# One stream of w_in blocks over three stages of a decoder trunk, with the next part's first weights prepared in the part before

## The reference

```
xn = rmsnorm(h);  proj = xn @ w_in                # 1024 x (3072 gates | 3328 RWKV | 1024 S5 | 2048 z, 3072 xBC, 32 dt)
o_r = rwkv7(...) ; o_s = s5(...) @ w_out_s5 ; o_m = mamba2(...) @ w_out_mamba
h  += rmsnorm((sig(g_r)*o_r + sig(g_s)*o_s + sig(g_m)*o_m) @ w_out)
mem_k, mem_v = rmsnorm(mem) @ xa_wk, rmsnorm(mem) @ xa_wv          # 256 memory tokens, both are outputs
h  += rmsnorm(cross_attend(rmsnorm(h), mem_k, mem_v));  h += rmsnorm(relu(rmsnorm(h) @ w1)^2 @ w2)
```

## Time and profile before

| | |
|---|---|
| time, median of 3 runs | 4400.95 us (4399.07 to 4402.61) |
| the profiled execution's own time | 4397.52 us |
| its span (first to last instruction of the profile) | 4395.8 us |
| PE busy | 4044.1 us, 92% |
| DVE, ACT, POOL busy | 2481.2, 1482.6, 156.8 us |
| mean DMA traffic | 95 GB/s |

### The profile page before, as it was taken

The page is one execution under the profiler, slowest core; times in us unless marked ns, Lnnn a source line. Parts: engine busy times, 40 slices in busy tenths (PEclk is TensorE's granted clock), DMA queues, the critical chain, the costliest instruction groups (busy, mean ns, idle before and its releaser), DMA issues. The chain is left out here.

```text
span 4395.8 us, 84548 instructions
## 1 busy us (share of the span) xinstructions
PE 4044.1 (92%) x35797; PEld 3722.4 (85%) x35797; DVE 2481.2 (56%) x5010; ACT 1482.6 (34%) x2684; POOL 156.8 (4%) x153
## 2 busy tenths in 40 slices
PE   8789999999989999889969999969988899999998
PEld 4789999989978888789957777759977889999997
DVE  3345646332278886358857777746552355444446
ACT  2113222221177553334324444424531352111112
POOL 0000000000001111000000000000012000000000
PEclk9899999989999999999979999979999999999999
DMA  5323232243355554556631010024313131111102
GB/s 181 89 86 90 87 90 91 74 104 102 107 157 148 154 144 124 165 149 204 197 118 33 25 32 30 25 93 144 100 63 103 45 107 58 47 46 44 49 29 80
DMA packets 374263, 418.69 MB, mean 95 GB/s; under 512 B 49162, under 2 KB 315964, under 8 KB 373020
## 3 DMA queue, kind: packets, MB, share of 16 engines
q1 hardware_dynamic: 361599, 368.01, 27.5%
q0 software_dynamic: 7680, 27.97, 2.2%
q10 hardware_dynamic: 4608, 17.30, 1.0%
HBM read 289.10 MB, written 121.77 MB: 93 GB/s over the span
## 5 line engine op out<-in xcount | busy, mean ns | idle before, releaser
L210 PE MATMUL bank<-xn_hi,pz_whi 128*128 128x352 f32 (+1 forms) x984 | 326.6, 332 | 15.2 <-DVE pz_wlo L195 14.6
L210 PE MATMUL bank<-xn_hi,pz_wlo 128*128 128x352 f32 (+1 forms) x984 | 319.8, 325 | 0.0
L210 PE MATMUL bank<-xn_lo,pz_whi 128*128 128x352 f32 (+1 forms) x984 | 318.0, 323 | 0.0
L3063 PE MATMUL bank<-bx_hi,bp_whi 128*128 128x384 f32 (+1 forms) x768 | 274.2, 357 | 29.8 <-DVE bx_lo L3121 18.5
L223 ACT ACTIVATE ring<-bank 128x352 f32<-128x352 f32 (+1 forms) x273 | 125.7, 462 | 519.0 <-PE bank L210 518.5
L1717 PE MATMUL bank<-sum_x_hi,sum_w_hi 128*128 128x352 f32 x768 | 254.2, 331 | 47.5 <-DVE sum_x_lo L1700 44.8
L210 PE MATMUL bank<-xn_hi,pb_whi 128*128 128x352 f32 x816 | 273.4, 335 | 17.6 <-DVE pb_wlo L195 13.0
L210 PE MATMUL bank<-xn_lo,pb_whi 128*128 128x352 f32 x816 | 264.9, 325 | 0.0
L210 PE MATMUL bank<-xn_hi,pb_wlo 128*128 128x352 f32 x816 | 264.0, 324 | 0.0
L3684 PE MATMUL bank<-bx_hi,bp_whi 128*128 128x384 f32 (+1 forms) x768 | 251.2, 327 | 4.7 <-issue 4.7
L3684 PE MATMUL bank<-ml_hidden_hi,bp_whi 128*128 128x384 f32 (+1 forms) x768 | 254.4, 331 | 0.0
(11 more groups left out here) (695 smaller groups left out, 12115.9 us busy)
## 6 DMA issues: line engine op xcount, KB each, us to landing
ring<-in_w_in_dram SPq DMA_DIRECT2D x90, 512.0 KB, 4.7
proj_scratch<-ring SPq DMA_DIRECT2D x66, 528.0 KB, 3.0
m_seg<-acum_scratch SPq DMA_DIRECT2D x32, 512.0 KB, 7.0
ring<-in_mlp_w_dram SPq DMA_DIRECT2D x16, 1024.0 KB, 5.5
ring<-in_mlp_w_dram SPq DMA_DIRECT2D x32, 512.0 KB, 3.5
gates_scratch<-ring SPq DMA_DIRECT2D x24, 528.0 KB, 5.1
merged_scratch<-sum_gate ACTq DMA_DIRECT2D x24, 528.0 KB, 5.6
m_raw<-proj_scratch SPq DMA_DIRECT2D x24, 512.0 KB, 5.3
```

The source lines that it names most:

```text
L210: last = self.nc.tensor.matmul(ps[0:n, 0:m], w[:, q, 0:n], self.pair[x][:, q, t0:t0 + m], start=q == 0 and j == 0, stop=q == KD - 1 and j ...
L3063: last = self.nc.tensor.matmul(ps, w[:, hu % 4, q, :], self.pair[x][:, 4 * hf + q, t0:t0 + m], start=hf == 0 and q == 0 and i == 0, stop=h ...
```

## The change

One `Columns` object now holds all three parts (91 blocks) and the first two weights of `Sums`. Its semaphores are kept over the stages' ends (`k.keep`, freed by `release_kept` after `branch_sums`), and so are the hi and lo tiles (`split`, names `pw_whi`, `pw_wlo`). `begin(part, pace)` chooses the part that a stage runs. Block b of the next part is loaded, and the first one also split, inside the stage of the part before. The first two blocks of all are loaded during the S5 input (`prime_load`). The waits for stores at the end of the first two parts go; `mamba_first` begins with `settled`.

In `Sums` the x loads come before the remaining weights, and the first chunk of x goes in two halves of four k tiles (`early_in`, `early_hi`, `early_lo`). In `S5Input` the first eight pieces of weights are loaded at the end of `front` instead, and the prompt rows are stored before the wait for the sample rows. `FrontMemory` writes keys and values into row buffers that exist already, and its yields and stores are put in another order.

```diff
+    def fetch(self, sp, b):
+        sp.dma_start(self.raw[:, b % 2, :, 0:self.width(b)], self.W[b].rearrange("(t p) n -> p t n", p=P)).then_inc(self.loaded[b % 2], 16)
     def load(self, sp):
-        for b, (W, _, _) in enumerate(self.blocks):
+        for b in range(self.first + 2, self.last + 2):
             yield self.at(b - 2, 0.2)
-            if b >= 2:
-                sp.wait_ge(self.w_lo, b - 1)
-            sp.dma_start(...)
+            sp.wait_ge(self.w_lo, b - 1)
+            self.fetch(sp, b)
+    def prime_load(self, sp, us, freed, count):
+        yield us
+        sp.wait_ge(freed, count)
+        for b in range(2):
+            self.fetch(sp, b)
+    def settle(self, sp, b):
+        for s in range(2):
+            sp.wait_ge(self.stored[s], 16 * ((b + 1 - s) // 2))
+    def settled(self, sp):
+        yield -100
+        self.settle(sp, self.first)
     def store(self, sp):
...
-        yield self.at(len(self.blocks) + 2)
-        for s in range(2):
-            sp.wait_ge(self.stored[s], 16 * ((len(self.blocks) + 1 - s) // 2))
+        if self.last == len(self.blocks):
+            yield self.at(self.last + 2)
+            self.settle(sp, self.last)
     def high(self, act):
-        for b in range(len(self.blocks)):
-            yield self.at(b - 1, 0.5)
+        for b in range(self.first + 1 if self.first else 0, self.last + 1):
+            yield self.at(b - 1, 0.5) if b else -50
# S5Input.sync
-        for s in range(2):
-            for q in range(KD):
-                sp.dma_start(self.raw[:, s, q, :], self.k.w_in[q * P:(q + 1) * P, C_S + s * 512:C_S + (s + 1) * 512]).then_inc(self.loaded[s], 16)
+        for q in range(KD):
+            sp.dma_start(self.raw[:, 1, q, :], self.k.w_in[q * P:(q + 1) * P, C_S + 512:C_S + 1024]).then_inc(self.loaded, 16)
         for s in range(2):
             yield self.at(s, Q5 + 2)
+            sp.wait_ge(self.off, 9 * s + Q5)
+            sp.dma_start(self.k.u_dram[:, 4 * s:4 * s + 4, :], ...).then_inc(self.stored, 16)
             sp.wait_ge(self.off, 9 * (s + 1))
-            sp.dma_start(self.k.u_dram[:, 4 * s:4 * s + 4, :], ...).then_inc(self.stored, 16)
# mamba_first
-                weave(columns.load(sp), columns.store(sp), steps.sync(sp), samples.sync(sp))
+                weave(columns.settled(sp), columns.load(sp), columns.store(sp), steps.sync(sp), samples.sync(sp))
# Sums.load_x
-                sp.dma_start(self.xraw[:, e % 2, :, :], src[:, :, t0:t0 + m]).then_inc(self.x_in[e % 2], 16)
+                if e == 0:
+                    sp.dma_start(self.xraw[:, 0, 0:4, :], src[:, 0:4, t0:t0 + m]).then_inc(self.early_in, 16)
+                q0 = 0 if e else 4
+                sp.dma_start(self.xraw[:, e % 2, q0:, :], src[:, q0:, t0:t0 + m]).then_inc(self.x_in[e % 2], 16)
# FrontMemory.sync
         for v, name in enumerate(("mem_k_prompt", "mem_v_prompt")):
+            if v:
+                yield self.START[3] + 4
+                sp.wait_ge(self.k_off, 4)
+                sp.dma_start(self.k.key_dram, self.keyT[:, :, :]).then_inc(self.out, 16)
+                sp.wait_ge(self.product, 6)
+                for q in range(KD):
+                    sp.dma_start(self.raw[:, 0, q, :], self.k.w_in[q * P:(q + 1) * P, C_S:C_S + 512]).then_inc(self.k.s5_first, 16)
             yield (self.START[2], self.START[3] + 16)[v] + 2
             sp.wait_ge(self.p_off, 4 * (v + 1))
             sp.dma_start(o[name][0, 0]..., self.made[v][:, :, :]).then_inc(self.out, 16)
-        yield self.START[3] + 20
-        sp.wait_ge(self.k_off, 4)
-        sp.dma_start(self.k.key_dram, self.keyT[:, :, :]).then_inc(self.out, 16)
         yield 1001
         sp.wait_ge(self.out, 48)
# FrontMemory.tensor, the key transposes
-            yield self.START[3] + 15 + 0.9 * g
+            yield self.START[2] + 14.2 + 0.4 * g
```

More of the change, by code:

```diff
@@ L55, in release, with release_kept @@
     k.sems.clear()
+def release_kept(k):
+    k.sems.extend(k.kept)
+    k.kept.clear()
+    release(k)
 def chunks3(t0=0, n=NT):
@@ L143, with __init__ @@
 class Columns:
[L146 to L148 removed]
+    def __init__(self, k, pair, parts, follow, split, banks):
+        self.k, self.nc, self.pair, self.banks = k, k.nc, pair, banks
+        self.blocks = [b for part in parts for b in part]
+        self.edges = [sum(len(part) for part in parts[:i]) for i in range(len(parts) + 1)]
+        self.W = [b[0] for b in self.blocks] + follow
+        S = lambda n: k.keep(f"pw_{n}")
         self.loaded, self.stored = [S(f"loaded{s}") for s in range(2)], [S(f"stored{s}") for s in range(2)]
         self.w_hi, self.w_lo, self.product, self.off = S("w_hi"), S("w_lo"), S("product"), S("off")
[L151 removed]
+        self.hi, self.lo = split
         flat = k.ring[:, :, :].rearrange("p a n -> p (a n)")
@@ L190, in low @@
     def low(self, dve):
-        for b in range(len(self.blocks)):
-            yield self.at(b - 1, 0.9)
+        for b in range(self.first + 1 if self.first else 0, self.last + 1):
+            yield self.at(b - 1, 0.9) if b else -49
             dve.wait_ge(self.w_hi, b + 1)
@@ L197, in multiply @@
     def multiply(self, pe):
-        for b in range(len(self.blocks)):
+        for b in range(self.first, self.last):
             n, hi, lo = self.width(b), self.hi[:, b % 2], self.lo[:, b % 2]
@@ L214, in evacuate @@
     def evacuate(self, act):
-        for b, (_, _, func) in enumerate(self.blocks):
-            n = self.width(b)
+        for b in range(self.first, self.last):
+            n, func = self.width(b), self.blocks[b][2]
             for c, (t0, m) in enumerate(chunks3()):
@@ L2128, in _ @@
             def _(sp):
-                weave(sums.weights(sp), sums.load_x(sp), sums.previous(sp), sums.gates(sp))
+                weave(sums.load_x(sp), sums.weights(sp), sums.previous(sp), sums.gates(sp))
             @block.gpsimd
@@ L2568, in vector, with mamba_first @@
         last.then_inc(self.normed, 1)
-def mamba_first(k, m, pair, blocks):
+def mamba_first(k, m, columns):
     nc = k.nc
@@ L4032, in __init__ @@
         self.rows, self.memT, self.keyT = sb("rows", [P, 2, D]), sb("memT", [P, KD, 256]), sb("keyT", [P, KD, 256])
-        self.made = [sb("key", [P, 2, D]), sb("val", [P, 2, D])]
+        self.made = [self.rows, rows]
         self.sq, self.rstd = self.made[0][:, :, :].rearrange("p a n -> p (a n)"), sb("rstd", [P, 256])
```

152 lines of the change are left out of this document (95 added, 57 removed).

## The result

The changed kernel takes 4360.65 us, median of 4 runs (4357.18 to 4363.08), against 4401.17 before: a ratio of 0.9908, 95% interval 0.9891 to 0.9925. That is 40.5 us sooner, where 18.7 were predicted and 31 was the end of the range.

What follows compares the result with a forecast made beforehand. PE, busy 92%, was taken as the bound, with time to gain only in its pauses at stage starts (82 us). Terms -2.7 + 8.2 + 2.8 + 6.2 + 4.2 gave 18.7 us sooner: 4382 median, range 4370 to 4393.

Steps and rivals of the forecast that it cites:

- A: Front's end to S5 input: values' store waits behind keys' store and 2 MB of weights; a loss of 2.7 us.
- B: S5 input to pz: prompt rows stored earlier and weights already there, so PE starts sooner; a gain of 8.2 us.
- C: pz to pa, mamba_first: third chunk still waits for the evacuation behind the step sizes; a gain of 2.8 us.
- sign for a short wait: mamba_first: no PE wait of about 5 us on the evacuation would mean a gain of 4.6 to 8 us.
- D: pa to pb: hi and lo are ready, so PE starts at the stage's first issue; a gain of 6.2 us.
- E: pb to output products: first half chunk of x goes first, third chunk gated by x; a gain of 4.2 us.
- both rivals for the third chunk: branch_sums: third x's lo ends at 1822.7, or a cold second chunk ends at 1823.4; gain 3.9 to 4.6 us.
- Kept semaphores and fewer tiles cost nothing in time.: Whole kernel: keeping semaphores and having fewer tiles was priced at no time.
- the five terms: The stage-start changes A, B, C, D and E, together 18.7 us sooner.
- Rival 1: All gaps close: values' store does not wait, pa restarts warm; 34 us sooner, 4367; chance 0.13 including what lies towards it.
- Rivals 2 and 3: Gates bind harder, 9 us sooner, 4392 (0.20 with half the other's price); or slower through the front's one queue (0.03).

## Why the prediction was wrong

**What bounds the kernel, and what the change does to it: right.** Every pause named in the earlier trace rows moved as said, and no new bound came up.

**A: right, 3.4 for 2.7.** The store behind the loads is what held the stage; moved ahead, the stage began 7.5 sooner. In the sum, the lighter traffic was called "worth 0 to 2 more" and then taken at 2.1. Measured, the stage began 9.1 later; its issues up to the last state rows took 5.0 less and those rows landed 0.7 sooner (16.07 and 4.44 before, 11.03 and 3.77 after): 5.7 back, where 6.1 was used. The rule on ring order of the Trainium skill (DMA: Bandwidth & Descriptors, Queues, rings and completion order) agrees with the trace: the values' store, issued at 115.49 behind 2 MB, landed 7.7 us later by the DMA view, 4.1 before:

```profile
out_mem_v_prompt_dram<-ft_rows SPq DMA_DIRECT2D x1, 1024.0 KB, 7.7
```

```profile
out_mem_v_prompt_dram<-fm_val SPq DMA_DIRECT2D x1, 1024.0 KB, 4.1
```

**B: right in its mechanism, 9.0 for 8.2.** The small store to the next stage's first work took 2.6 us (250.01 to ACT's 252.61) and not 3.3. The restart is cold, as said (a granted clock of 0.50 from 255 to 260).

**C: the mechanism right, the size wrong, 7.2 for 2.8.** The term that was mis-sized is "From issue to L2298 took 6.75, about 0.9 of it DVE busy with other things past the landing. So L2298 at 895.4 or a little sooner (less traffic)". I kept 5.8 from issue to chain; it measured 3.35. The landing time had 1 MB of weights directly ahead of it, which the change removes, and I took away their issue time (1.01) but not their share of the landing (5.0 against 2.4). This alone is 2.4 of the 4.4. Most of the rest follows from it: PE hardly waited, so its third chunk took 4.1 us (884.73 to 888.85) and not the cold 5.7. That the weights ahead made the landing late is shown by the run with the small loads first, 2.3 in place of 5.0, in one execution. The prediction's own sign for a short wait ("no such wait means 4.6 to 8") fits the 7.2.

**D and E: right**, 6.25 for 6.2 and 4.6 for 4.2. In E both rivals for the third chunk, the x chain and the cold second chunk, were close to each other, as estimated.

**The sum: this is where it failed.** "Kept semaphores and fewer tiles cost nothing in time." This term was put at nothing, with no row read for it. The tiles' places were a change of their own. Of the 15 us outside the five terms, 6.8 are in pz and are shown by the runs with the order of the kernel before: 616.5 and 617.2 with tiles moved far, 618.35 with 32 bytes. In time these runs gain 0.17 to 0.19% each, nearly half of what the prediction gave to all five terms. So two steps failed: this term, 6.8 for 0, and the landing in C, 3.35 from issue to chain for 5.8. About 4.7 more are spread over the other stretches that share the weight tiles or their neighbours; the runs do not separate them from scatter. The last 3.5 lie behind the sums in code that the change leaves alone, though tiles moved there too. It varies by more than that between programs and runs, so they are not explained.

**The rivals.** Rival 1, all gaps close, named 34 us, nearer to the outcome than my forecast, but half for the wrong reason: A did not close, C nearly did. Rivals 2 and 3 did not come up.

## What to carry to other kernels

A change that keeps tiles alive over stages also moves every tile above them: compare the mean time of the commonest matmul before and after, apart from the pauses, before a gain is put down to the order of work. A landing time read from a trace can include what was queued directly ahead (here 5.0 us with two weight loads ahead, 2.3 without); if the change removes that, the time goes with it. And here the store that ends a stage belonged ahead of the next stage's prefetches, and loads that are needed late behind the parameters that are needed first: PE's restart in the S5 input came 5.9 and 5.1 us sooner by these two moves.

## What the runs showed of the hardware

Matmuls of 128x352 in fp32r ran at 332 and 325 ns (mean, with the hi and the lo weights) with both weight tiles at a multiple of 64 bytes in the partition, and at 328 and 324 with the tiles 32 bytes further, at a granted clock of 1.00 in both; the stretch that holds them was 5.5 us shorter (the kernel before, and the run with the 32-byte shift). For tiles low in the buffer the same step cost 2.7 to 3.1 us in the order of the kernel before (616.5 to 619.6 and 619.2), and 2.2 in the changed kernel (617.1 to 619.3). So the offset modulo 64 is a cause, and not the only one: at a multiple of 64 the tiles at the top were slower than low ones (623.9 and 624.9 against 619.6 and 619.2), at 32 past one hardly (618.35 against 616.5 and 617.2). Why is open.

The clock can fall after a pause that is over. In mamba_first PE paused only 2.1 us, with 1.00 granted in it, and the low clock came after its restart:

```profile
872.10:874.19 2.09, 0.00 (x1) 0.03 (x1) 0.10 (x2) 0.57 (x2) 0.00 (x0) 1.00 0.29 65
874.19:876.20 2.01, 2.01 (x9) 2.01 (x10) 1.57 (x4) 1.99 (x2) 1.43 (x5) 0.71 0.03 4
876.20:880.00 3.80, 3.80 (x19) 3.80 (x19) 2.04 (x4) 1.17 (x3) 0.68 (x1) 0.70 0.83 149
```

A mean of 0.7 over the last two stretches is a mixture of 1.00 and 0.50 (2.4 and 1.2 GHz), while PE was never idle. The timeline of PE shows the matmuls start 0.16 us apart up to 875.07, 0.29 apart from there to 878.29, and 0.16 apart behind it. The first two chunks took 9.45 us together (874.19 to 883.64) in place of the 7.7 that the prediction used. That loss cost nothing: PE waited for the evacuation anyway, 1.09 us in place of the 2.8 that it would have waited with chunks of 7.7. In branch_sums it was the same after a pause of 2.99 us: the second chunk started 0.16 apart at 1788.47 and ran 0.29 apart from 1789.88 to 1793.10.
